# Summing half of the weighted expert rows of the tail chunks on TensorE instead of VectorE

## The reference

```python
s = jnp.einsum('chpd,hpnd->chpn', q, sub_keys)          # scores of the sub-keys
...                                                     # two top-16s give eidx and best
g = jax.nn.softmax(best, axis=-1)
act = jax.nn.gelu(jnp.einsum('chkd,cd->chk', u_tab[eidx], x))
return jnp.einsum('chk,chkd->cd', (g * act), v_tab[eidx])
```

## Time and profile before

| | us |
|---|---|
| median of three runs | 2827.2 (2824.89 to 2843.02) |
| the profiled execution, own time | 2830.05 |
| its span, first to last instruction | 2828.2 |
| DVE busy in the span | 2272.4 |
| POOL busy | 1480.3 |
| PE busy | 1039.5 |
| ACT busy | 276.9 |

### The profile page before, as it was taken

One profiled execution on the slowest core, in us unless ns is written; L12 is line 12 of the kernel. 1 busy time (PEld: TensorE's weight loads), 2 busy tenths in 40 slices (PEclk: granted clock), 3 DMA queues, 4 the chain that ended last, 5 costly groups with the idle time before them and its releaser, 6 DMA issues.

```text
span 2828.2 us, 15862 instructions
## 1 busy us (share of the span) xinstructions
PE 1039.5 (37%) x4071; PEld 632.8 (22%) x4071; DVE 2272.4 (80%) x3923; ACT 276.9 (10%) x569; POOL 1480.3 (52%) x1284
## 2 busy tenths in 40 slices
PE   6788659999777978960000000000000000000000
PEld 2578534444355455430000000000000000000000
DVE  1432577976887785998998999979999998888999
ACT  0441204530032000000000000000000000000000
POOL 0000002336435560006887777787777778777774
PEclk9899779999888988985555555555555555555555
DMA  8667446579856982106989999998999999999997
GB/s 281 199 219 244 132 136 214 185 238 349 304 181 233 362 299 92 60 0 237 329 304 327 360 346 362 361 320 309 363 364 379 356 371 334 363 375 369 389 409 307
DMA packets 310359, 803.49 MB, mean 284 GB/s; under 512 B 23230, under 2 KB 142830, under 8 KB 310260
## 3 DMA queue, kind: packets, MB, share of 16 engines
q0 software_dynamic: 184320, 671.17, 64.7%
q1 hardware_dynamic: 125948, 131.31, 14.2%
HBM read 799.44 MB, written 2.94 MB: 284 GB/s over the span
## 4 chain that ended last, share of the span: by engine, by line
POOL 37%; DVE 20%; issue 18%; PE 15%; DMA 5%; ACT 3%; DVEq 1%; SPq 0%; ACTq 0%
POOL big L1481 36%; PE bank L586 10%; ACT work L809 2%; PE bank L570 2%; DMA h_all<-in_peer_u_dram,eidx 2%; DMA ring_more<-in_peer_u_dram,eidx 1%; PE bank L760 1%; DVE mix_region L1414 1%; DVE mix_region L1411 1%; DVE mix_region L1410 1%; DVE mix_region L1413 1%; DVE work L1282 1%; DVE mix_region L1459 1%; DVE work L1412 1%; DVE h_all L1100 1%
## 5 line engine op out<-in xcount | busy, mean ns | idle before, releaser
L1481 POOL DMA_INDIRECT big<-in_peer_u_dram,eidx x512 | 619.0, 1209 | 397.9 <-DVEq L1191 227.7
L586 PE MATMUL bank<-big 128*128 128x128 f32 (+1 forms) x2336 | 683.6, 455 | 61.4 <-DVEq L1009 30.2
L1459 DVE SCALAR_TENSOR_TENSOR mix_region<-big,gw,mix_region 128x1024 f32<-128x1024 f32 x512 | 652.7, 1294 | 46.9 <-DMA big<-in_peer_v_dram,eidx 41.4
L1453 DVE CUSTOM_DVE_ANT_0 big<-big,h_all 128x1024 f32<-128x1024 f32 x512 | 622.3, 1226 | 57.8 <-DMA big<-in_peer_u_dram,eidx 55.3
L1481 POOL DMA_INDIRECT big<-in_peer_v_dram,eidx x512 | 565.0, 1104 | 156.5 <-issue 155.5
L586 PEld LDWEIGHTS bank<-big 128*128 128x128 f32 x2336 | 377.4, 204 | 354.9 <-issue 332.7
L1481 POOL DMA_INDIRECT h_all<-in_peer_u_dram,eidx x78 | 90.7, 1163 | 552.3 <-DVEq L1432 416.5
L1481 POOL DMA_INDIRECT h_all<-in_peer_v_dram,eidx x76 | 88.4, 1163 | 74.5 <-DVE gf_row L1109 41.7
L1100 DVE CUSTOM_DVE_ANT_0 h_all<-h_all 128x1024 f32<-128x1024 f32 x78 | 94.9, 1223 | 17.5 <-DMA h_all<-in_peer_u_dram,eidx 14.4
L1481 POOL DMA_INDIRECT ring_more<-in_peer_v_dram,eidx x52 | 61.2, 1178 | 75.7 <-DVE gf_row L1109 37.1
L809 ACT ACTIVATE work<-bank 128x512 f32<-128x512 f32 (+2 forms) x104 | 47.5, 457 | 463.2 <-DVEq L1306 205.0
(11 more groups left out here) (180 smaller groups left out, 1379.8 us busy)
## 6 DMA issues: line engine op xcount, KB each, us to landing
big<-in_w_in_dram SPq DMA_DIRECT2D x44, 1024.0 KB, 6.9
big<-in_w_ada_dram SPq DMA_DIRECT2D x24, 1024.0 KB, 7.9
big<-in_peer_w_q_dram SPq DMA_DIRECT2D x16, 1024.0 KB, 5.5
big<-in_w_rnn_o_dram SPq DMA_DIRECT2D x8, 1024.0 KB, 8.9
big<-in_w_attn_o_dram SPq DMA_DIRECT2D x8, 1024.0 KB, 7.3
big<-in_w_out_dram SPq DMA_DIRECT2D x8, 1024.0 KB, 13.0
big<-in_peer_u_dram,eidx POOLq DMA_INDIRECT x512, 6.2
big<-in_peer_v_dram,eidx POOLq DMA_INDIRECT x512, 6.3
```

Source lines behind the costliest of these rows:

```text
L586: last = nc.tensor.matmul(u[:, 0:n], w[:, k, col:col + P], src[:, k, 0:n], start=(k == 0), stop=(k == KD - 1))
L1453: V.tensor_tensor_reduce(ring[r], ring[r], h2_all[:, c, :], 1.0, 0.0, ALU.mult, ALU.add, dots[:, k:k + 1]).then_inc(row_used, 1)
L1459: V.scalar_tensor_tensor(acc[k % 2], ring[r], gw[:, c, k:k + 1], acc[k % 2], ALU.mult, ALU.add)\
L1481: g.indirect_dma_start(dst, None, ins["peer_" + table][0], bass.IndirectOffsetOnAxis(ap=eidx[:, c, k:k + 1], axis=0)).then_inc(landed, 16)
```

## The change

In steps 1 to 4 every v row with an even k goes to TensorE, the odd ones stay on VectorE; u rows stay as they are. For a row on TensorE, ScalarE writes a diagonal matrix with the row's weights per token (identity times `gw[:, c, k]`) into one of four 128 x 128 buffers (`diag`), and TensorE multiplies it with the two halves of the row in the ring buffer, 128 x 512 each, adding up 64 such products in two PSUM banks per chunk (two others for the next chunk). At a chunk's end VectorE adds the two banks to its accumulator (`add_peer`) before what it did until now. GpSimd waits for the engine that used the buffer before, VectorE or TensorE. ScalarE writes the diagonals of k below 72 before the Exp of the next chunk's routing, the rest behind it.

```diff
+    turns = [(*step[n % len(step)], n // len(step)) for step in steps for n in range(len(step) * SLOTS)]
+    for table, _, k in turns:
+        by.append("tensor" if table == "v" and k % 2 == 0 else "vector")
...
+            for turn, (table, c, k) in enumerate(turns):
+                if by[turn] != "tensor":
+                    continue
+                r, n = turn % RING, count_after[turn]
+                if k == 0 and c - C1 >= 2:
+                    pe.wait_ge(sums_free, c - C1 - 1)
+                pe.wait_ge(diag_ready, n)
+                pe.wait_ge(row_in[r], 16 * (turn // RING + 1))
+                for i in range(2):
+                    last = nc.tensor.matmul(psum[2 * (c % 2) + i][:, :], diag[:, (n - 1) % DIAGS, :],
+                                            ring[r][:, i * 512:(i + 1) * 512], start=(k == 0), stop=(k == SLOTS - 2))
+                last.then_inc(row_used["tensor"], 1)
+                if k == SLOTS - 2:
+                    pe.drain().then_inc(sums_full, 1)
...
+            def diags(c, k0, k1):
+
+                for k in range(k0, k1, 2):
+                    n = ((c - C1) * SLOTS + k) // 2
+                    if n >= DIAGS:
+                        act.wait_ge(row_used["tensor"], n - DIAGS + 1)
+                    run(diag[:, n % DIAGS, :], ident[:, :], ACT.Identity, scale=gw[:, c, k:k + 1]).then_inc(diag_ready, 1)
...
+                for c in v_chunk:
+                    act.wait_ge(gw_ready, c - C1 + 1)
+                    diags(c, 0, SOFT_AT)
+                if u_chunk and u_chunk[0] + 1 < NCH:
+                    soft(u_chunk[0] + 1)
+                for c in v_chunk:
+                    diags(c, SOFT_AT, SLOTS)
...
+            def add_peer(c):
+
+                dve.wait_ge(row_used["vector"], sums_at[c])
+                dve.wait_ge(sums_full, c - C1 + 1)
+                for i in range(2):
+                    link(V.tensor_tensor(acc[0][:, i * 512:(i + 1) * 512], psum[2 * (c % 2) + i][:, :],
+                                         acc[0][:, i * 512:(i + 1) * 512], ALU.add))
+                chain.wait()
+                dve.drain().then_inc(sums_free, 1)
+                add_sums(c, acc)
...
-                    else:
-                        if k >= 2:
-
-                            dve.wait_ge(row_used, turn + 1 - 2 * len(step))
-                        V.scalar_tensor_tensor(acc[k % 2], ring[r], gw[:, c, k:k + 1], acc[k % 2], ALU.mult, ALU.add)\
-                            .then_inc(row_used, 1)
+                    elif by[turn] == "vector":
+                        r, a_ = turn % RING, acc[k // 2 % 2]
+                        if k >= 4:
+
+                            dve.wait_ge(row_used["vector"], count_after[turn - 4 * len(step)])
+                        dve.wait_ge(row_in[r], 16 * (turn // RING + 1))
+                        V.scalar_tensor_tensor(a_, ring[r], gw[:, c, k:k + 1], a_, ALU.mult, ALU.add)\
+                            .then_inc(row_used["vector"], 1)
...
-                    if turn >= RING:
-                        pool.wait_ge(row_used, turn - RING + 1)
-                    fetch(table, c, n // len(step), ring[r], row_in[r])
-                    turn += 1
+                if turn >= RING:
+                    pool.wait_ge(row_used[by[turn - RING]], count_after[turn - RING])
+                fetch(table, c, k, ring[r], row_in[r])
```

More of the change, by code:

```diff
@@ L295, in hybrid_step @@
         pq_sb = [wk(0), wk(1)]
+        diag = work[:, 0:DIAGS * P].rearrange("p (i n) -> p i n", i=DIAGS)
         cut = wk(2)
@@ L1470, in _ @@
                     if table == "v":
-                        add_sums(c, acc)
+                        add_peer(c)
                         final(c, acc[1])
```

55 lines of the change are left out of this document (29 added, 26 removed).

## The result

| | us |
|---|---|
| the kernel after, median of 20 runs | 2795.3 (2774.3 to 2822.9) |
| the kernel before, median of 20 runs beside them | 2823.7 (2794.3 to 2846.3) |
| ratio after / before, 95% interval | 0.9916 [0.9892, 0.9941] |
| the profiled execution of after, own time | 2774.3 |
| its span | 2772.4 |

What follows compares the result with a forecast made beforehand. GpSimd's issuing of expert rows, held up by VectorE's instructions, was taken to bound the tail. Steps 1 to 3 -53, boundaries +3, end -4: -54 us, from a median of 2827.2 to 2773 us; range 2726 to 2842.

Steps and rivals of the forecast that it cites:

- rival C: Last step: TensorE stays at 1.2 GHz and becomes the bound, 243 us instead of 164; 2856 us in all, chance 0.08.
- The backlog: Mixed steps: VectorE works off rows landed in free time; 36 rows gone in 63 us instead of 171.
- x = 1.36: Mixed steps: us per row issued by GpSimd while VectorE waits for landings, 1.43 before; saves 53 us over steps 1 to 3.
- waiting stretches: Parts of the mixed steps in which VectorE is idle between landings; 1.43 us a row before, 1.36 forecast.
- 0.75 x 0.19: Waiting VectorE: GpSimd's hold-up of 0.19 us a row falls with the number of VectorE's instructions to 0.14, giving 1.38 a row.
- the pause over the TensorE row: Waiting VectorE: where the TensorE row stands, a pause of over a us lets a GpSimd issue pass.
- 45 + 63 + 184x: Steps 1 and 2: free time, backlog, then 184 rows at x us; 358 us each against 376 modelled before.
- rival A: Mixed steps: no relief while VectorE waits, 1.43 us a row or a bit more; 2815 to 2840 us, chance 0.24.
- 12 + 18 + 236x: Step 3, without routing: boundary, backlog, then 236 rows at x us; 351 us against 368 modelled before.
- rival B: Mixed steps: full relief, issues fall into step with landings 1.28 us apart; 2726 us, chance 0.12.
- The end: End of the last step: VectorE finishes one instruction behind the last landing, then two additions of 1.5 us; saves 4 us.
- The boundaries' +3: Boundaries inside the tail: two additions of 1.5 us and the wait for TensorE's last row cost 3 us over all.

Runs made afterwards that it cites:

- e1: The kernel before, with VectorE's instruction on each u and v row of the tail replaced by a one-input tensor_reduce of nearly the same length: 2672.7 us, ratio 0.9466.
- e3: The kernel after, with TensorE multiplying only the first and last of its rows per chunk and passing on the other 62 buffers: 2794.4 us, ratio 0.9896.
- e14: The kernel after, unchanged, run for a third profile: 2801.4 us.
- e8: The kernel after, unchanged, run for a second profile: 2798.0 us.
- e7: The kernel after, with all four parts of the routing done at once at the step's start: 2823.1 us, ratio 0.995.
- e13: The kernel after, with only VectorE's v additions cut in two of 512 columns, u instructions whole: 2826.1 us, ratio 0.9946.
- e12: The kernel after, with only VectorE's u instructions cut in two of 512 columns, v additions whole: 2703.8 us, ratio 0.9612.

## Why the prediction was right and wrong

**Right: what bounds the tail.** GpSimd's issues are held up by VectorE's instructions, and the transfers have room up to 410 GB/s. e1 shows the first by itself, and the windows of after the second (398 GB/s in step 3, 405 in step 4). The 358 GB/s that the prediction quotes from the Trainium skill ("SBUF — State Buffer", A bandwidth-pool intuition that's wrong) are no limit here.

**Right: TensorE, ScalarE and the order of things.** e3 removes the matmuls and changes nothing. In step 4 the granted clock is 1.00 and a row takes 1.96 us every 2.56, so rival C falls. The backlog behaves as it was worked out: counted from the end of each routing part or boundary to VectorE's next wait for a landing, it lasts 57 to 62 us in all in steps 1 and 2 of the three traces (forecast 63). Only for before was it taken too long, 171 us where the same count gives 138 and 147. Timeline of after, behind a routing part in step 1:

```profile
1610.56 0.93 POOL L1536 DMA_INDIRECT big<-in_peer_u_dram,eidx  x1 [0.30 <-issue]
1611.74 1.21 DVE L1505 CUSTOM_DVE_ANT_0 big<-big,h_all 128x1024 f32<-128x1024 f32 x1
1611.80 1.96 POOL L1536 DMA_INDIRECT big<-in_peer_v_dram,eidx  x1 [0.30 <-issue]
1612.88 1.22 DVE L1505 CUSTOM_DVE_ANT_0 big<-big,h_all 128x1024 f32<-128x1024 f32 x1
1614.03 1.29 DVE L1513 SCALAR_TENSOR_TENSOR mix_region<-big,gw,mix_region 128x1024 f32<-128x1024 f32 x1
1614.06 0.93 POOL L1536 DMA_INDIRECT big<-in_peer_u_dram,eidx  x1 [0.30 <-issue]
```

Two issues from 1610.56 to 1614.06, 3.50 us, where 3.51 was forecast: one gets in at the v row, the other is held by the first of the two u rows.

**Wrong: the one rate x = 1.36 of the waiting stretches, from "0.75 x 0.19" and the pause over the TensorE row.** It took the hold-up to go with the number of VectorE's instructions, the same in every step. Put the measured steps into the forecast's own formula, 45 + 63 + 184x for steps 1 and 2: the means of 377.4 and 381.8 us give x = 1.46 and 1.49, which is rival A's band and a little over it. Some of that isn't the rate: the free stretches took 50 and 56 us, not 45, and in them a full ring stopped GpSimd for 6 and 12 us. Counted in the waiting stretches alone, the issues of the three traces are 1.44 and 1.43 us apart in steps 1 and 2. That is the 1.43 which the forecast had for before (counted likewise, before has 1.52 and 1.41), so there was hardly any relief: rival A was right there. Step 3 comes to 1.32 either way (12 + 18 + 236x from 342.1 us, or counted), half way from the forecast to rival B's 1.28.

There are two paces, and the forecast 1.36 stands between them. The first is that of step 3 of after from 2339 us to the step's end, and of steps 1 and 2 only from 1549 to 1611 and from 1928 to 1989 us, behind the boundary and up to the next routing part. (e14 has it there in step 1 alone and e8 in neither step.)

```profile
2440.08 0.94 POOL L1536 DMA_INDIRECT big<-in_peer_v_dram,eidx  x1 [0.30 <-issue]
2440.21 1.23 DVE L1505 CUSTOM_DVE_ANT_0 big<-big,h_all 128x1024 f32<-128x1024 f32 x1 [1.34 <-DMA big<-in_peer_u_dram,eidx]
2441.33 0.93 POOL L1536 DMA_INDIRECT big<-in_peer_u_dram,eidx  x1 [0.30 <-issue]
2441.56 1.28 DVE L1513 SCALAR_TENSOR_TENSOR mix_region<-big,gw,mix_region 128x1024 f32<-128x1024 f32 x1
2442.57 1.09 POOL L1536 DMA_INDIRECT big<-in_peer_v_dram,eidx  x1 [0.30 <-issue]
2442.76 1.22 DVE L1505 CUSTOM_DVE_ANT_0 big<-big,h_all 128x1024 f32<-128x1024 f32 x1
2443.96 0.94 POOL L1536 DMA_INDIRECT big<-in_peer_u_dram,eidx  x1 [0.30 <-issue]
2445.21 0.93 POOL L1536 DMA_INDIRECT big<-in_peer_v_dram,eidx  x1 [0.31 <-issue]
```

Each issue begins 0.13 to 0.23 us ahead of an instruction of VectorE, or meets a pause; the worst is held for 0.15. Four go in 5.13 us (2440.08 to 2445.21), 1.28 each. It looks as if rows then land evenly, VectorE starts evenly, and the pattern keeps itself up; the runs show that it lasts (12 stretches of 16 rows in this trace's step 3), not what keeps it. The other pace, in step 2:

```profile
2134.35 1.02 POOL L1536 DMA_INDIRECT big<-in_peer_u_dram,eidx  x1 [0.30 <-issue]
2135.19 1.22 DVE L1505 CUSTOM_DVE_ANT_0 big<-big,h_all 128x1024 f32<-128x1024 f32 x1 [0.63 <-DMA big<-in_peer_u_dram,eidx]
2135.67 1.55 POOL L1536 DMA_INDIRECT big<-in_peer_v_dram,eidx  x1 [0.30 <-issue]
2137.53 0.94 POOL L1536 DMA_INDIRECT big<-in_peer_u_dram,eidx  x1 [0.30 <-issue]
2138.19 1.23 DVE L1505 CUSTOM_DVE_ANT_0 big<-big,h_all 128x1024 f32<-128x1024 f32 x1 [1.77 <-DMA big<-in_peer_u_dram,eidx]
2138.77 1.46 POOL L1536 DMA_INDIRECT big<-in_peer_v_dram,eidx  x1 [0.31 <-issue]
...
2140.53 1.11 POOL L1536 DMA_INDIRECT big<-in_peer_u_dram,eidx  x1 [0.30 <-issue]
```

The issue at 2135.67 starts inside the u row of 2135.19 and takes 1.55; the one at 2138.77 starts inside the next u row and takes 1.46. Presumably a held issue makes its row land late, a later instruction start late and the next issue meet it again. Four issues from 2134.35 to 2140.53 in 6.18 us make 1.54 each; in stretches of 16 rows behind the backlogs this pace is 1.31 to 1.48 in steps 1 and 2. In before such stretches are mostly 1.32 to 1.5, and 1.28 never lasts for more than one of them (1.27 from 2155 us, 1.29 from 2246).

Steps 1 and 2 are interrupted by a routing part every 64 turns, and after each come a free stretch, a backlog and a search for the pattern. With the routing all at the start (e7) both steps have 1.28 for some 120 us in one piece, late in the step, where the first trace of after has it for 60 us early on. This speaks for the parts within the step as what breaks the pattern, but doesn't prove it: step 1 of e7 lost the pattern with no routing near, and e13's step 3 never found it. What makes it lock, 54 us into step 1 of after and 276 us into step 2 of e7, stays open.

**The rate was read off the wrong thing.** The 0.19 us was counted over u and v rows alike. e12 and e13 part them: halving the u rows gives all but 7 us of what halving both does (2703.8 and 2696.9), halving the v rows nothing, though they are a third of the rows that VectorE has. The prediction had the sign of this in its hands: u rows alone go at 1.64 us, slower than the mixed steps, and rival A named the two u rows side by side. For steps 1 and 2 it was the better forecast, at a chance of 0.24.

**The smaller terms.** The end: 28.7 us from the last issue before, 20.3 to 21.0 after, -8 for the forecast -4. Timeline of after at the end, which answers to the earlier trace rows:

```profile
2751.40 1.01 POOL L1536 DMA_INDIRECT big<-in_peer_v_dram,eidx  x1 [0.30 <-issue]
...
2758.64 1.28 DVE L1513 SCALAR_TENSOR_TENSOR mix_region<-big,gw,mix_region 128x1024 f32<-128x1024 f32 x1 [1.18 <-DMA big<-in_peer_v_dram,eidx]
2759.96 1.42 DVE L1485 TENSOR_TENSOR mix_region<-bank,mix_region 128x512 f32<-128x512 f32 x2
2761.59 1.23 DVE L1172 TENSOR_TENSOR mix_region<-mix_region 128x1024 f32<-128x1024 f32 x1 [0.21 <-DVE mix_region L1485]
```

The last row is followed at once by the two additions, 1.42 us and a gap of 0.21 (forecast 1.5). But step 4 grew by 6 us, which was forecast at nothing: before, GpSimd ran 1.24 us a row ahead of the DMA engines and left them a queue; after, it goes in step with them. So step 4 and the end together give -2 us (-4 forecast). The boundaries' +3 agree in size: GpSimd's stop before a full ring at the start of step 2 went from 8.8 to 12.5 us.

**In sum**: -9 for steps 1 and 2 (forecast -36), -31 for step 3 (-17), -2 for the last (-4), the boundaries within the steps, and +3 in step 0, which the change doesn't touch. Two errors partly cancel, too much in two steps and too little in one; that the total of the traces (-39 for -54) misses by less than its largest part is luck, not insight. The range (2726 to 2842) holds the result. Of the signs that were named, VectorE's idle time grew (97 to 345 us) and held issues became rarer (185 to 120 in steps 1 to 4), but issues 1.33 to 1.40 us apart in waiting stretches are in none of the mixed steps' means.

## What to carry to other kernels

Where GpSimd issues DMAs beside a VectorE that streams two-input instructions, look at the mean of the issues in the profile against the shortest: here 1.21 against 0.94 us (the u issues of before take 619.0 us for 512) was worth 5% of the kernel. The cheap remedy is the length of VectorE's instructions, not their number: the same work in pieces of 512 columns, the u rows above all, with one row in four moved to TensorE so that VectorE can afford the cut, gives 2694 us, 4.6% under before and 3.6% under after. And where a producer and a consumer disturb each other, don't forecast one mean rate: look for stretches in which they run in step, and at what interrupts them.
